# Tangent for sigmoid and silu, one-column totals, and a new order of some tiles in a fused four-layer fp32 kernel

## The reference

```python
for l in range(2):
    h = rms_norm_2(x, norm_g[l])
    (pool_u, pool_z, aq, ak, av, az, iq, ik, iw, mq, mz, gates) = split(h @ w_in[l])
    y_pool = multi_scale_pool(pool_u, pool_w[l], pool_scale[l]) * silu(pool_z)
    y_attn = dsa_attention(aq, ak, av, iq, ik, iw, rel_bias) * silu(az)
    y_mem  = memory_attention(mq, *split(rms_norm_2(mem, mem_norm_g[l]) @ w_mem_kv[l])) * silu(mz)
    g = sigmoid(gates).reshape(b, s, 3, 1024)
    merged = (g[:, :, 0] * (y_pool @ w_branch[l, 0]) + g[:, :, 1] * (y_attn @ w_branch[l, 1])
              + g[:, :, 2] * (y_mem @ w_branch[l, 2]))
    x = x + merged @ w_out[l]
return rms_norm_2(x, final_g)
```

## Time and profile before

| | us |
|---|---|
| median of three timed runs | 1624.4 |
| profiled execution, whole | 1628.06 |
| its span | 1626.3 |
| TensorE busy | 1581.7 |
| VectorE busy | 1104.0 |
| ScalarE busy | 947.2 |
| GpSimd busy | 348.0 |
| mean granted clock | 0.96 |

### The profile page before, as it was taken

One profiled execution on the slowest core, in us unless ns is written; L12 is line 12 of the kernel. 1 busy time (PEld: TensorE's weight loads), 2 busy tenths in 40 slices (PEclk: granted clock), 3 DMA queues, 4 the chain that ended last, 5 costly groups with the idle time before them and its releaser, 6 DMA issues.

```text
span 1626.3 us, 35018 instructions
## 1 busy us (share of the span) xinstructions
PE 1581.7 (97%) x14201; PEld 1486.6 (91%) x14201; DVE 1104.0 (68%) x2253; ACT 947.2 (58%) x1990; POOL 348.0 (21%) x412
## 2 busy tenths in 40 slices
PE   7999999979999999999999999999999999999999
PEld 6988898969899999988899999889899989898998
DVE  4777677666488864756789955766666667676663
ACT  6765456535376653546386654547676554667754
POOL 5232123414033321001323311000402210040010
PEclk9998699989799999999799999999999999999999
DMA  5322021314265554443366766545345656444452
GB/s 207 117 80 80 27 93 53 100 59 145 85 209 174 178 173 143 131 129 104 104 186 186 198 208 195 168 132 168 117 143 168 201 162 198 141 147 153 139 174 90
DMA packets 64976, 230.41 MB, mean 142 GB/s; under 512 B 7312, under 2 KB 9488, under 8 KB 64816
## 3 DMA queue, kind: packets, MB, share of 16 engines
q1 hardware_dynamic: 59792, 217.67, 42.5%
q0 software_dynamic: 4160, 8.98, 1.8%
q10 hardware_dynamic: 864, 1.52, 0.3%
HBM read 222.91 MB, written 5.24 MB: 140 GB/s over the span
## 4 chain that ended last, share of the span: by engine, by line
PE 83%; DVE 7%; ACT 4%; issue 4%; POOL 2%; DMA 1%; SPq 0%; ACTq 0%; POOLq 0%
PE ps L690 80%; PE ps L694 3%; DVE splitL L2373 3%; DVE arena L2381 2%; ACT splitH L1767 1%; POOL sq L3197 1%; ACT arena L1772 1%; DVE mixT L2378 1%; DMA ring<-wst 1%; ACT arenaR L1772 1%; DVE mixT L2381 0%; ACT L1772 0%; DVE arena L2378 0%; DVE arena L2385 0%; ACT sq L1772 0%
## 5 line engine op out<-in xcount | busy, mean ns | idle before, releaser
L2373 DVE TENSOR_TENSOR splitL<-ring,splitH 128x512 fp32r<-128x512 f32 x767 | 561.5, 760 | 232.8 <-ACT splitH L1767 224.2
L690 PE MATMUL ps<-aH,splitH 128*128 128x256 f32 (+2 forms) x2232 | 665.4, 299 | 7.2 <-ACT aH L1772 5.4
L690 PE MATMUL ps<-aH,splitL 128*128 128x256 f32 (+2 forms) x2232 | 641.3, 288 | 0.0
L690 PE MATMUL ps<-aL,splitH 128*128 128x256 f32 (+2 forms) x2232 | 627.1, 287 | 0.0
L1767 ACT ACTIVATE splitH<-ring 128x512 fp32r<-128x512 f32 x824 | 480.6, 623 | 128.2 <-PE ps L690 114.9
L690 PEld LDWEIGHTS ps<-aH,splitH 128*128 128x128 f32 x2232 | 430.4, 193 | 23.3 <-issue 12.3
L690 PEld LDWEIGHTS ps<-aH,splitL 128*128 128x128 f32 x2232 | 430.8, 193 | 0.0
L690 PEld LDWEIGHTS ps<-aL,splitH 128*128 128x128 f32 x2232 | 422.4, 192 | 0.5
L690 PE MATMUL ps<-arenaR,splitH 128*128 128x256 f32 (+2 forms) x1856 | 350.9, 289 | 3.1 <-POOL arenaR L3197 2.0
L690 PEld LDWEIGHTS ps<-arenaR,splitH 128*128 128x128 f32 x1856 | 293.0, 192 | 6.0 <-POOL arenaR L3197 1.9
L690 PE MATMUL ps<-arenaR,splitL 128*128 128x256 f32 (+2 forms) x928 | 265.2, 286 | 0.0
(11 more groups left out here) (212 smaller groups left out, 1309.2 us busy)
## 6 DMA issues: line engine op xcount, KB each, us to landing
ring<-wst SPq DMA_DIRECT2D x412, 512.0 KB, 3.9
mem_scratch<-arenaR POOLq DMA_DIRECT2D x16, 128.0 KB, 3.7
arenaR<-mem_scratch POOLq DMA_DIRECT2D x4, 512.0 KB, 8.6
rel_scratch<-arena POOLq DMA_DIRECT2D x8, 255.5 KB, 4.8
arena<-x SPq DMA_DIRECT2D x2, 512.0 KB, 5.0
arena<-mem POOLq DMA_DIRECT2D x2, 512.0 KB, 4.4
arena<-rel_scratch POOLq DMA_DIRECT2D x1, 1024.0 KB, 9.7
out<-arena ACTq DMA_DIRECT2D x4, 256.0 KB, 2.1
```

The source lines that it names most:

```text
L690: return pe.matmul(out, lhsT, rhs, start=start, stop=stop)
L2373: dve.tensor_tensor(lo, raw, hi.bitcast(F32), ALU.subtract).then_inc(*inc(("lo_dve", q)))
```

## The change

1. Second block: silu(x) is x/2 (1 + tanh(x/2)) and sigmoid(x) is (1 + tanh(x/2))/2. ScalarE writes tanh(x/2), VectorE multiplies (one plus it) by the PSUM tile; the factors 1/2 go into instructions that exist already. The z tiles' banks are freed by VectorE and no longer by ScalarE. The planner counts Exp and Tanh as one table.
2. f1 gets `mix_sums` like f0 and ml, with six added tiles in place of five; the totals, layings out, scalings, adds and cuts are set at given steps of the memory tiles (`beside`). x0 gets one-column totals of its squares. `stat`, `mix_out`, `root`, `residual` and `norm` go.
3. Down projections: tiles 0 to 2 go together, k 0 to 19 of each, then k 20 and 21 of each.
4. Order of the branches (`MERGE`): gate tile 0, pooling products, gate tile 1, branch tiles 0 and 1, then pairs as before.

```diff
-TABLES = (ACT.Exp, ACT.Ln, ACT.Sqrt, ACT.Silu, ACT.Sigmoid, ACT.Tanh)
+TABLES = {ACT.Exp: 0, ACT.Tanh: 0, ACT.Ln: 1, ACT.Sqrt: 2, ACT.Silu: 3, ACT.Sigmoid: 4}
+def beside(steps, at):
+    for i, _ in enumerate(steps):
+        if i in at:
+            at[i]()
+        yield
+        ADDED = {"gdn": 5, "f0": 5, "ml": 5, "f1": 6}
+        DOWN = (0, 20, 22)
+        MERGE = [("g", 0, 0), ("pw", 0, 0), ("g", 0, 1), ("b", 0, 0), ("b", 0, 1)]
+        MERGE += [(x, br, m) for br in range(3) for m in range(KD) if br or m > 1 for x in ("g", "b")]
...
# TensorE, mix_sums
+                at = {3: range(3)} if ADDED[name] == 5 else {K - 8 + 3 * q: (q,) for q in range(3)}
...
# TensorE, ffn
-                repay()
                 give_back()
-                yield from (mix_sums if name == "f0" else mix_out)(
-                    name, ("ffn_w_down", layer), NF, both(fH[:, :, drop:n], fL[:, :, drop:n], n - drop), n - drop, need2)
+                down, mid = ("ffn_w_down", layer), both(fH[:, :, drop:n], fL[:, :, drop:n], n - drop)
+                for m, k in in_turn(NF, DOWN):
+                    if m >= 3:
+                        break
+                    if k == 0:
+                        fg.get(name, m)
+                    h, l, end = take(128, (*down, k * 128, 128 * m, 128))
                     w.wait_ge("fLp", name, k)
+                    t = mm3(ps(name, m)[:, 0:n - drop], h, l, mid(k), k == 0, k == NF - 1)
...
+                yield from mix_sums(name, down, NF, mid, n - drop, lambda k, part="lo": None, first=3)
+                if name == "f0":
+                    repay()
...
# TensorE, second
                 if l == 0:
-                    for k in range(KD):
-                        stat("xn0", k, ("sqa", "xn0", k // 2), N, start=k == 0, stop=k == KD - 1)
+                    yield from beside(memory(), {5: lambda: totals("f1", N), 11: lambda: first_scale("f1", N),
+                                                 16: lambda: second_scale("xn0", N)})
+                    scaled("f1", "xn0")
+                    repay()
                 else:
-                    stat("x0", 7, ("sqp", "x0", 7), N, buf=mixT, stop=True)
+                    borrow(2)
+                    yield from beside(memory(), {4: first_total, 8: last_total, 20: scale})
...
-                        if k == KD - 1 and l == 0:
-                            if m in (2, 4, 6):
-                                stat("x0", m - 2, ("sqm", "x0", m - 2), N, buf=mixT, start=m == 2)
-                            if m == 7:
-                                stat("x0", 6, ("sqa", "x0", 6), N, buf=mixT)
...
# ScalarE, second
-                                a(dst[:, m, :], ps(name if name[-1] in "01" else name + str(l), m)[:, 0:N], f).then_inc(*inc((name.rstrip("01") + "a", l, m)))
+                                a(dst[:, m, :], ps(name if name[-1] in "01" else name + str(l), m)[:, 0:N], ACT.Tanh if gated else ACT.Copy,
+                                  scale=0.5 if gated else 1.0).then_inc(*inc((name.rstrip("01") + "a", l, m)))
-                                a(gate[ng % 2], ps(f"g{l}{br}", m)[:, 0:N], ACT.Sigmoid)
+                            a(gate[ng % 2], ps(f"g{l}{br}", m)[:, 0:N], ACT.Tanh, scale=0.5)
+                    yield from beside(memory(), {5: lambda: first_root("f1", N), 12: lambda: second_root("f1", "xn0", N)} |
+                                      {25 + 2 * j: lambda j=j: high("xn0", j, N) for j in range(4)})
...
# VectorE, second
+                def gated(name, dst):
+                    for m in range(4):
+                        for k in range(KD):
+                            feed.take(128)
+                            if k == KD - 1:
+                                w.wait_ge(name + "a", l, m)
+                                stt(dst[:, m, :], dst[:, m, :], 1.0, ps(name + str(l), m)[:, 0:N], ALU.add, ALU.mult)
+                            yield
+                    yield from beside(memory(), {6: lambda: reciprocal("f1", N), 8: lambda: energy("f1", N),
+                                                 13: lambda: second_reciprocal("xn0", N)} |
+                                      {14 + 3 * j: lambda j=j: scaled(j) for j in range(4)} |
+                                      {25 + 2 * j: lambda j=j: normed("xn0", j, N, xT, "ng2", 0) for j in range(4)} |
+                                      {28 + 4 * j: lambda j=j: low("xn0", 2 * j, N) for j in range(2)})
...
-                                    tt(sq[:, m, 0:N], b, gate[ng % 2], ALU.mult)
+                                stt(sq[:, m, 0:N], gate[ng % 2], 1.0, b, ALU.add, ALU.mult)
-                            tt(xT[:, m, :], ps(f"x{l}", m)[:, 0:N], xT[:, m, :], ALU.add)
+                            stt(xT[:, m, :], ps(f"x{l}", m)[:, 0:N], 0.5, xT[:, m, :], ALU.mult, ALU.add)
```

More of the change, by code:

```diff
@@ L1676, in second @@
+                    yield from dense(f"b{l}{br}", ("w_branch_2", l, br), [128 * m], 4, both(yH[br], yL[br], N), N, yneed,
+                                     lambda m: [("bm", l, br, m)], m0=m)
                 give_back()
@@ L2502, in mix_sums @@
                     yield
-            def mix_out(K):
-                for m in range(KD):
-                    for k in range(K):
-                        feed.take(128)
-                        yield
             def gates():
@@ L3058, in tokens, with memory, scaled @@
                         yield
-                if l == 0:
-                    root("f1", N)
-                yield from four_(f"mk{l}", mkT, (0, 1))
-                if l == 0:
-                    residual("f1", "xn0", N, xT)
-                yield from four_(f"mk{l}", mkT, (2, 3))
-                if l == 0:
-                    norm("xn0", N)
-                else:
-                    norm("x0", N, xg)
-                yield from tokens("mv", mvt)
+                def memory():
+                    yield from four_(f"mk{l}", mkT)
+                    yield from tokens("mv", mvt)
+                def scaled(j):
+                    scale("f1", "xn0", j, N)
+                    add("xn0", j, N, xT)
+                if l == 0:
+                    yield from beside(memory(), {6: lambda: reciprocal("f1", N), 8: lambda: energy("f1", N),
[3 more added lines that the diff above has]
+                                      {28 + 4 * j: lambda j=j: low("xn0", 2 * j, N) for j in range(2)})
+                else:
+                    yield from beside(memory(), {13: lambda: reciprocal("x0", N)} |
+                                      {22 + 3 * j: lambda j=j: second_norm(j) for j in range(4)} |
+                                      {26 + 6 * j: lambda j=j: low("x0", 2 * j, N, xg) for j in range(2)})
                 for _ in range(KD):
@@ L3406, in second, with memory @@
                     pool.dma_start(bias1, skew(127, 256)).then_inc(*inc(("bias",), by=16))
-                yield from plain(2 * KD)
+                def memory():
+                    yield from plain(4 * KD)
+                    yield from plain(KD, 512)
                 if l == 0:
-                    residual("f1", "xn0", N, xT, "ng2", 0)
-                yield from plain(2 * KD)
-                if l == 0:
-                    norm("xn0", N)
-                else:
-                    norm("x0", N, xg)
-                yield from plain(KD, 512)
+                    yield from beside(memory(), {28 + 4 * j: lambda j=j: low("xn0", 2 * j + 1, N) for j in range(2)})
+                else:
+                    yield from beside(memory(), {29 + 6 * j: lambda j=j: low("x0", 2 * j + 1, N, xg) for j in range(2)})
                 for _ in range(2 * KD):
```

538 lines of the change are left out of this document (239 added, 299 removed).

## The result

The changed kernel takes 1616.9 us in the median of 13 runs (1605.8 to 1623.0), the kernel before 1624.4 (1619.5 to 1629.6): ratio 0.994, 95% interval 0.992 to 0.996. Repeated later (12 runs) it was 1613.8 us, again at 0.994 (0.991 to 0.997). The medians differ by 7.5 us here and 8.3 us in the repeat; the ratios, which go by all runs, make it 9 to 10, where 12 were forecast. One execution of the kernel before took 6889 us and is left out everywhere.

What follows compares the result with a forecast made beforehand. TensorE, busy 97% of the span, was taken as the bound. Gains of 3.8 + 1.1 + 5.4 + 1.6 = 11.9 us off the median 1624.4 gave 1612.5, forecast as 1612 us, range 1602 to 1624.

Steps and rivals of the forecast that it cites:

- rival A: Attention tasks woven anew, waits move: pooling-product move and tangent give only 1 us, total 1618.5 us; chance 0.22.
- part 1, down: f1's down projection: grouping three tiles removes waits for GpSimd, restarts and half clock behind them; gain 3.8 us.
- part 2, f1: One-column totals replace full sums at f1: work grows by 1.1 us, waits shrink by 1.4; gain 0.3 us.
- part 2, x0: One-column totals at x0: 2.8 us added against 2.2 of sums and a 1.38 us wait removed; gain 0.8 us.
- part 3, MERGE: Layer 0's pooling products behind a gate tile: 3.5 us hole shrinks to 1 us at full clock; gain 5.4 us.
- layer 1, with part 4: Layer 1's waits of 1.05, 0.39 and 0.69 us, 2.1 in all, mostly go; gain 1.6 us.
- part 4, tangent: Second half: 60 us of table loads off ScalarE are hidden; 24 added VectorE products, 11.5 us, cost nothing.
- Rival C: VectorE's order becomes the bound through 24 gated products: 20.6 us if all shows, total 1640.1 us; chance 0.11.
- The signs named in the prediction: No idle near 941, 47 table loads, layer 0's pooling holes at most 1.5 us without half clock, unbroken f1 totals.
- wrong signs: Holes before `tin` or `sums` matmuls, splits released late in the z tiles, or half clock after f1.
- rival B: One-column totals at the memory tiles bring half clock once or twice, about 1.5 us each; total 1615; chance 0.07.
- D: Every hole closes and totals cost their lower bounds: 16.8 us gained, total 1607.6 us; chance 0.14.

Runs made afterwards that it cites:

- e1: Changed kernel with the down projections' first three tiles one after another again: 1617.5 us, ratio 0.995 to the kernel before.
- e4: Changed kernel with grouped down tiles, moved pooling products and tangent undone, so only the one-column totals remain: 1618.5 us, ratio 0.998 to the kernel before.
- the square: Second-block times of e2, e3, e4 and the changed kernel (mean 557.9 us), compared with and without moved pooling products and with and without the tangent.
- e12: Kernel before, with only the planner pricing Exp and Tanh as one table, so attention tasks stand elsewhere: 1622.2 us, ratio 1.001 to the kernel before.
- e8: Changed kernel with each of the 24 gated z-tile products done twice on VectorE, TensorE's order kept: 1616.1 us, ratio 0.997 to the kernel before.
- e6: Changed kernel with VectorE's twelve small pooling operations behind the second zm product, TensorE's order kept: 1612.3 us, ratio 0.992.
- e7: Changed kernel with silu and sigmoid as functions again, TensorE's order kept: 1621.2 us, ratio 0.999 to the kernel before.
- e2: Changed kernel with the pooling products ahead of the first gate tile again, tangent kept: 1616.7 us, ratio 0.996.
- e3: Changed kernel with silu and sigmoid as functions again and the planner's table prices too (47 more table loads): 1615.0 us, ratio 0.993.
- e11: Changed kernel with the tangent for the 48 gate tiles only, silu as a function for the 24 z tiles: 1612.7 us, ratio 0.994 to the kernel before.
- e10: Kernel before, unaltered, profiled again to see what a profile repeats: 1622.1 us, ratio 1.001.
- e5: Changed kernel with the planner pricing a table load between Exp and Tanh again, so only the task order differs: 1615.5 us, ratio 0.995.

## Why the prediction was right, and where it was not

The direction and the range were right; the time was 5 us too low by the first median (1612 against 1616.9), 2 by the second. The first median lies 0.6 us above the 1616.3 that the prediction set as the bound of "faster", the second below it. That the sum came so near is in part luck: two errors went opposite ways. The totals gave 4.7 us in place of 1.1, and parts 3 and 4 with layer 1 together 1.8 in place of 7.0. By its parts, rival A (parts 3 and 4 give 1 us) fits the second block better than the forecast does. Means of the profiles, stages only:

```
                     forecast   measured
part 1, down          -3.8      -2.5, and -1.5 in some runs   (after against e1)
part 2, f1            -0.3      -2.5                          (e4 against before)
part 2, x0            -0.8      -2.2, with the order it made; -0.9 to -1.3 by its rows
part 3, MERGE         -5.4      -3.4 to -3.8, in layer 1      (the square)
layer 1, with part 4  -1.6      in part 3
part 4, tangent        0        +1.6 to +2.0                  (the square)
sum                  -11.9      -9.0, or -10.5 with the clock of part 1
```

- **Part 1** was right in place and mechanism; its clock term comes in some executions only.
- **Part 2** was undersized. The step that failed is the price of what was added at f1, 6.7 us where 4.5 were measured: a laying out (0.8 us taken; it is 0.36, under the lower bound), a one-column total, taken from a row with two tiny groups beside the two large ones (0.6; it is 0.36 to 0.49), and a frame (0.38; it is 0.26 to 0.31). The waits of 0.41, 0.97 and 1.38 us went; in one of two profiles of the changed kernel a wait of 0.50 stands at x0.
- **Part 3, layer 0**: the hole of 3.5 us and its half clock went, as forecast, but not for the forecast's reason. The step that failed is to count the removal of a hole as the gain of an edit when the same edit makes the planner lay the tasks anew. One line of the planner moves that hole to layer 1 (e12) and gains nothing in the second block; the totals alone, with the new order that they brought, did the same (e4). What MERGE gains stands in layer 1 above all (258.9 to 253.7 with functions, where a hole of 3.55 us and the half clock behind it go; 258.3 to 256.1 with the tangent, by half clock alone, and for that row luck isn't excluded).
- **Layer 1, with part 4**: forecast 1.6 less, measured 2.3 more. Two holes of 1.67 and 0.88 us took the place of the three of the earlier trace rows. The matmuls of the attention and memory tasks also stand more finely between the others: 134 changes from one kind to the other against 126 before, and the distances from start to start within and around them sum to 42.6 us against 40.6, holes left out.
- **Part 4** "hidden" failed on both sides. The loads cost 7.4 us if they come back into this order, most of it by half clock, and nothing if the order is made for them; the products on VectorE are not covered (e8), with 0.62 us of loss for each us added. Rival C named the engine and its queue, with 20.6 us as its price; a cost of a tenth of that is what the square shows. That the loss of e8 comes through the clock and not through waits was not in it.
- **The signs named in the prediction**: no idle near 941, four loads after f1's down and 47 in all, no hole over 1.5 us and no half clock at layer 0's products, dense steps unbroken at f1's totals: all seen. Of the wrong signs one came, the half clock after f1 (rival B), in three of eleven profiles at 1.6 us.
- **Rival A** was right in kind: e6 and e7 show a wait closed at one place and given back at the next. **D** did not come as a whole, but its term for the totals (4.5 us) did.

Open: what the order, what the products' place and what the clock's chance contributes to the 3.4 to 3.8 us of MERGE, since no version was run with the place changed and the order of the tasks kept, and e2, e3 and e4 have one profile each; and the microsecond of the 2.2 that stands in no row of x0.

## What to carry to other kernels

Where a planner lays out the work, a hole in the profile belongs to the plan as much as to the line at which it shows: change one price alone and look at whether the hole moves before counting it as gain. An operation moved to an engine that is 70% busy isn't free for that (e8); where a form without the extra operation exists, try it (tangent for the gates, function for the z tiles: e11, the shortest second block, though not clear of the changed kernel in whole times). And compare stages cut at the same work, with the time at half clock beside them: here 1 us was plain in a stage of equal clock, while whole executions of one kernel spread over 20 us.

## What the runs showed of the hardware

- One order of TensorE's instructions, 14 profiles: the first stage took 421.5 to 432.8 us with 48 to 79 us at 1.2 GHz, and over 103 executions of the kernel before the time follows the mean granted clock (0.957 to 0.972, 1633 to 1613 us, correlation -0.96). So most of the scatter of this kernel goes with its clock.
- A hole of equal length may or may not bring the clock down. After 1.67 us at 1441.6 the kernel after stays at full clock, and so do its repeat and e1 at the same place; after 1.67 us at 1450.0 e2 has 6.8 us at half clock, from 1452.0 on. In both orders the plain fp32 matmuls of an attention head stand among the dense ones behind the hole. Nor does the length alone decide: 2.38 us in e3 left the clock full, 1.30 us in e8 were followed by half clock. All four holes of about 3.5 us (before, e10, e12, e4) came with it. The hole at f1's down did it in three of five profiles. By the Trainium skill (TensorE: Matmul & The Clock Gate, "HAM oscillation — how this bites in real kernels") it is a long gap in TensorE's work that brings the clock down; here gaps of 1.3 to 2.0 us were followed by it, and so were the totals after f1 with no gap at all (e1, e5, e6).
- Operations added to VectorE cost TensorE time through the clock: TensorE's idle time in the second block stayed at 3.3 us, but 17 us were at half clock where the kernel after has none (e8).
